# One order of matmuls for every unit of weights in a two-block transformer kernel

## The reference, cut to what matters

```
first_block:  h += hybrid_mixer(rmsnorm(h))          # h @ w_in, SSD, convolutions, @ w_out
              h += memory_cross_attention(rmsnorm(h)) # w_q, w_k, w_v, w_o
              h += (silu(n @ w_gate) * (n @ w_up)) @ w_down        # n = rmsnorm(h), D_FF = 5632
second_block: x += concat(pool, hyena, gmlp)(n @ w_in_2) @ w_out_2
              up = dwconv3(n @ ffn_w_up_2);  gate, val = split(up)
              x += (silu(gate) * val) @ ffn_w_down_2
return rmsnorm(x)
```

## Time and profile before

| | us |
|---|---|
| median of three executions | 2719.59 (2719.28 to 2724.88) |
| profiled execution, its own time | 2724.14 |
| span in the profile, first to last instruction | 2722.4 |
| TensorE busy with matmuls | 2656.2, 14978 of them |
| VectorE busy | 1924.6 |
| ScalarE busy | 1495.8 |

### The profile page before, as it was taken

How to read it: one execution, slowest core, us unless ns; L and a number is a source line. 1 busy time by engine, 2 the same in 40 slices (tenths; PEclk the granted TensorE clock), 3 DMA queues, 4 the chain that set the end, 5 groups by cost and what they waited for, 6 DMA issues and landing times.

```text
span 2722.4 us, 38546 instructions
## 1 busy us (share of the span) xinstructions
PE 2656.2 (98%) x14978; PEld 2286.7 (84%) x14978; DVE 1924.6 (71%) x2916; ACT 1495.8 (55%) x2307; POOL 388.7 (14%) x391
## 2 busy tenths in 40 slices
PE   7999999999998999999999999999999999999997
PEld 7888888888887888888888878888888888888886
DVE  8776777777787665656565679687876767676775
ACT  6555566768555444444444456545555555555554
POOL 3011100403411000010101033011101010101012
PEclk9999999999998999999999999999999999999998
DMA  6555566656554555666666656536566666666663
GB/s 247 173 180 182 184 191 193 186 182 183 174 175 134 168 162 171 186 187 188 189 186 187 190 161 209 162 124 185 178 193 188 187 189 189 186 187 187 190 178 118
DMA packets 135838, 490.76 MB, mean 180 GB/s; under 512 B 15207, under 2 KB 15528, under 8 KB 135656
## 3 DMA queue, kind: packets, MB, share of 16 engines
q1 hardware_dynamic: 135656, 488.31, 59.2%
HBM read 486.12 MB, written 2.13 MB: 179 GB/s over the span
## 4 chain that ended last, share of the span: by engine, by line
PE 87%; DVE 8%; ACT 2%; issue 2%; DMA 0%; DVEq 0%; ACTq 0%; SPq 0%
PE ps L715 32%; PE ps L733 24%; PE ps L716 16%; PE ps L730 12%; DVE wl L1218 3%; ACT wh L936 1%; DVE hT L1218 1%; DVE X L1224 1%; PE ps L872 0%; PE ps L905 0%; DVE A L1224 0%; DVE T L1224 0%; DVE R L1218 0%; DVE Gf L1218 0%; DVE T L1218 0%
## 5 line engine op out<-in xcount | busy, mean ns | idle before, releaser
L1218 DVE TENSOR_TENSOR wl<-raw,wh 128x1024 fp32r<-128x1024 f32 x902 | 1139.7, 1268 | 723.9 <-ACT wh L936 722.6
L936 ACT ACTIVATE wh<-raw 128x1024 fp32r<-128x1024 f32 x902 | 952.4, 1059 | 967.2 <-PE ps L716 536.2
L733 PE MATMUL ps<-X,wh 128*128 128x512 f32 x2816 | 860.1, 396 | 2.8 <-DVE hT L1218 2.8
L715 PE MATMUL ps<-XG,wh 128*128 128x512 f32 x2304 | 827.3, 403 | 29.7 <-DVE hT L1218 16.4
L715 PE MATMUL ps<-X,wh 128*128 128x512 f32 x2032 | 725.2, 401 | 2.0 <-DVE wl L1218 1.3
L716 PE MATMUL ps<-XG,wl 128*128 128x256 f32 x2304 | 650.4, 282 | 0.0
L716 PE MATMUL ps<-X,wl 128*128 128x256 f32 x2032 | 568.7, 280 | 0.0
L730 PE MATMUL ps<-X,wl 128*128 128x256 f32 x2816 | 564.6, 281 | 0.0
L715 PEld LDWEIGHTS ps<-XG,wh 128*128 128x128 f32 x2304 | 436.8, 190 | 142.9 <-DVE hT L1218 21.8
L733 PEld LDWEIGHTS ps<-X,wh 128*128 128x128 f32 x2816 | 481.5, 189 | 71.9 <-issue 4.7
L730 PEld LDWEIGHTS ps<-X,wl 128*128 128x128 f32 x2816 | 484.6, 189 | 61.5
(11 more groups left out here) (172 smaller groups left out, 1313.6 us busy)
## 6 DMA issues: line engine op xcount, KB each, us to landing
raw<-in_w_gate SPq DMA_DIRECT2D x176, 512.0 KB, 3.7
raw<-in_w_down SPq DMA_DIRECT2D x176, 512.0 KB, 3.7
raw<-in_w_sc SPq DMA_DIRECT2D x96, 512.0 KB, 4.2
raw<-in_w_up SPq DMA_DIRECT2D x88, 512.0 KB, 3.7
raw<-in_w_val SPq DMA_DIRECT2D x88, 512.0 KB, 3.7
raw<-in_w_zx SPq DMA_DIRECT2D x80, 512.0 KB, 3.8
raw<-in_w_in SPq DMA_DIRECT2D x68, 512.0 KB, 3.8
raw<-in_w_osc SPq DMA_DIRECT2D x32, 512.0 KB, 3.7
```

The source lines that it names most:

```text
L715: e.matmul(bank(c, i)[:, :], W1, x, start=st and kk == 0, stop=False)
L733: t = e.matmul(bank(c, i)[:, :], wh[:, b0:b0 + 128], X[:, kx * 512:kx * 512 + 512], start=st and kk == 0, stop=sp and n == ends[i])
L936: return e.activation(out, in_, ACT.Copy, scale=scale)
L1218: return e.tensor_tensor(out, a, b, op)
```

## The change

In every unit, per tile of K: the 512-column matmuls of its banks, and then the 256-column ones (order 1 above). `ORDERS` and `ORDER_OF` are gone, and gate and up columns wait tile by tile like the others. The `v` columns, with three 256-column matmuls, keep their order; `dt` has one bank, so its order is the same.

```diff
             for kk in range(c.kn):
                 X, kx, s, n = xtile(c, g * c.kn + kk)
-                if kk == 0 or c.kind not in ("gate", "up"):
-                    w.wait_ge(s, xtile(c, g * c.kn + c.kn - 1)[3] if c.kind in ("gate", "up") else n)
+                w.wait_ge(s, n)
                 x = X[:, kx * 512:(kx + 1) * 512]
-                if c.kind in ("gate", "up"):
-                    continue
-                for i in range(nb):
-                    b0 = (u % NW) * UN + kk * c.w
-                    if c.kind != "v":
-                        W1, W2 = wh[:, b0 + 128 * i:b0 + 128 * i + 128], wl[:, b0 + 128 * i:b0 + 128 * i + 128]
-                        e.matmul(bank(c, i)[:, :], W1, x, start=st and kk == 0, stop=False)
-                        t = e.matmul(bank(c, i)[:, 0:256], W2, x[:, 0:256], start=False, stop=sp and kk == c.kn - 1)
...
-            if c.kind in ("gate", "up"):
-                order = ORDERS[ORDER_OF[c.i]]
-                ends = {i: n for n, (kk, i, low) in enumerate(order)}
-                for n, (kk, i, low) in enumerate(order):
...
+                else:
+                    for i in range(nb):
+                        e.matmul(bank(c, i)[:, :], wh[:, b0 + 128 * i:b0 + 128 * i + 128], x, start=st and kk == 0, stop=False)
+                    for i in range(nb):
+                        t = e.matmul(bank(c, i)[:, 0:256], wl[:, b0 + 128 * i:b0 + 128 * i + 128], x[:, 0:256], start=False,
+                                     stop=sp and kk == c.kn - 1)
             t.then_inc(mm, 1)
```

More of the change, by code:

```diff
@@ L383, in schedule @@
     return at
[L387 to L394, removed]
 PLAN = schedule()
@@ L705, in unit @@
                 X, kx, s, n = xtile(c, g * c.kn + kk)
-                if kk == 0 or c.kind not in ("gate", "up"):
-                    w.wait_ge(s, xtile(c, g * c.kn + c.kn - 1)[3] if c.kind in ("gate", "up") else n)
+                w.wait_ge(s, n)
                 x = X[:, kx * 512:(kx + 1) * 512]
-                if c.kind in ("gate", "up"):
-                    continue
-                for i in range(nb):
-                    b0 = (u % NW) * UN + kk * c.w
-                    if c.kind != "v":
-                        W1, W2 = wh[:, b0 + 128 * i:b0 + 128 * i + 128], wl[:, b0 + 128 * i:b0 + 128 * i + 128]
-                        e.matmul(bank(c, i)[:, :], W1, x, start=st and kk == 0, stop=False)
-                        t = e.matmul(bank(c, i)[:, 0:256], W2, x[:, 0:256], start=False, stop=sp and kk == c.kn - 1)
-                    else:
-                        W1, W2 = wh[:, b0:b0 + 256], wl[:, b0:b0 + 256]
+                b0 = (u % NW) * UN + kk * c.w
+                if c.kind == "v":
+                    W1, W2 = wh[:, b0:b0 + 256], wl[:, b0:b0 + 256]
+                    for i in range(2):
                         xh, xl = x[:, i * 128:i * 128 + 128], x[:, 256 + i * 128:384 + i * 128]
```

## The result

The changed kernel took 2710.5 us (median of five, 2707.5 to 2710.9) against 2719.3 for the kernel before (five, 2717.6 to 2724.9): a ratio of 0.9962, with a 95% interval of 0.995 to 0.9975. Run again twice, it took 2707.2 and 2708.9 beside 2720.6 and 2718.8 (ratios 0.996, [0.9948, 0.9973], and 0.9957, [0.9945, 0.997]). All together, 16 executions have a median of 2708.5 and 56 of before one of 2719.5: 11 us, 0.4%. The forecast of 2704 lay 6.5 us too low, inside the range of 2696 to 2713 but just outside the likeliest case's own range of 2698 to 2710. Its profiled execution took 2710.54 us (span 2708.7), 13.6 less than that of before, where 16.0 was forecast.

The account below looks back on a forecast made before the run. TensorE's matmul spacing was taken as the bound. Gains of 11.2 us outside gate/up and 4.8 in gate/up sum to 16.0, turning the profiled 2724.1 into 2708.1; 4.5 less for unprofiled executions gives 2704, with an 8-in-10 range of 2696 to 2713.

Parts of the forecast that it names:

- the likeliest case: Whole kernel: the forecast of 2704 us itself, chance 0.80, with its own range of 2698 to 2710 for level mix and clock.
- What bounds the kernel: Whole kernel: TensorE is busy 98% of the span, so time is the sum of start-to-start spacings of matmuls.
- Order 1's pace: Four-unit gate/up columns of the kernel before: 2.787 us a unit, one level, taken to hold in all changed units.
- the 4.8: Gate/up units: sum of the gains from giving all of them the new order, 4.8 us.
- the other 494 gain 0.023 each: 11.2 us: Units outside gate/up where TensorE is the bound: from a mean of 2.810 to 2.787 us, 11.2 us in all.
- 4.5 less, so 2703.6: Whole kernel: unprofiled median lies 4.5 us below the profiled execution, so the profiled forecast of 2708.1 becomes 2703.6.
- two more or fewer: Idle places: two more or fewer half-clock stretches, 1.6 us each, move the time by 3 us.
- Only gate/up gains: Rival: down, out and mixer columns gain nothing, leaving 4.8 us; time 2714.8, chance 0.08.
- order doesn't matter: Rival: the levels belong to the stretch, not the order of matmuls; time stays at 2719.6, chance 0.04.
- slower by a high level: Rival: the new order also has a high level, 2.840 us a unit; time 2734 at the old share, chance 0.04.
- The bigger gain: Rival: the new order throughout finds 2.773 us a unit; some 850 units save 0.013 more, 11 us; 2693, chance 0.04.
- Order 0's mix: Undisturbed units outside gate/up, 512 and 256 columns alternating: 249 high at 2.827 us, 119 low at 2.7735, mean 2.810.

Follow-up runs that it names:

- the parts done alone: Two kernels against the one before: new order only outside gate/up, 2711.4 us (ratio 0.9968); new order and tile-wise waits only in gate/up, 2712.0 us (0.9974).
- order 0 alone: Against the changed kernel: every unit alternates 512- and 256-column matmuls, one bank after the other; median of 12 executions 2716.7 us, profiles 2730.8 and 2714.3.

## Why the prediction came out as it did

**What bounds the kernel** was right: the two long stretches stayed full and gave 8.2 of the 13.6 us; the rest came from undisturbed units elsewhere.

**Order 1's pace carried over** to other columns, operands and neighbours, as forecast: 2.787 everywhere, one level, also in the parts done alone. Taken unit by unit between the two first profiles, the 365 undisturbed units outside gate/up saved 8.5 us, 0.023 each as forecast, and the 323 in gate/up 4.7 us of the 4.8.

**The mis-sized term** is "the other 494 gain 0.023 each: 11.2 us". Nearly all of them did. Beside the undisturbed ones, some 110 run a foreign matmul, or the unit ahead of them does, without a wait and at full clock, and they saved 2.5 us, 0.023 each. What was left out are some 15 units with a wait or a half-clock stretch in one of the two profiles: together they lost 3.6 us, where 0.3 of gain was counted. Some 1.7 of that are longer waits, 0.57 of it in one unit near 721 us, for the residual add: TensorE gets there earlier and the add comes no sooner. The rest is the clock: a unit near 94 us met a half-clock stretch that before had not (1.57 us), and near 1810 us a stretch moved and a wait grew (0.35). The other way, a unit near 711 us, priced at nothing, was spared one that before had (1.55). So 16.0 became 13.6 between profiles.

**The other step that was off** is "4.5 less, so 2703.6": it carried the distance between before's profiled execution and its median over to the changed kernel. That distance was before's clock, 0.992 in the profiled execution and 0.994 in its middle ones. The changed kernel has 0.992 in its middle ones too, so its first profile lay on its median. At 0.992 the forecast for the profiled execution, 2708.1, meets a mean of 2709.4. The two errors, 2.4 and 4.5 us, together stayed inside the range, but the range's own term for the clock was too small: "two more or fewer" allowed 3 us, and executions of one kernel differ by six such stretches, 10 us.

**The rivals.** Only gate/up gains, order doesn't matter, and slower by a high level fell, by the down windows at 2.787. The bigger gain fell too: no stretch of order 1 went to 2.773. The waits per tile were worth nothing. Order 0's mix, which the first term took from one profile, came out nearly the same in before (119 and 113 low), partly by luck, as stretches changed both ways. It did not in order 0 alone (99 and 325 of some 690).

What stays open: why order 0 has two levels, and what decides after a disturbance which one a stretch takes; and why the changed kernel's executions had the lower clock. Order 1 outside gate/up alone had a mean of 0.9939 in eleven executions, and order 1 in gate/up alone 0.9936 in seven, so neither part brings it by itself; 16 executions don't exclude chance.

## What to carry to other kernels

Where matmuls of two sizes alternate, read the pace from start to start in windows of whole columns, for each order: equal work took 2.773, 2.787, 2.793 or 2.827 us a unit. Pairs of equal size gave one level in every profile, though not the shortest. A single profiled execution can lie 10 us from another of the same kernel by the clock alone, so compare the granted clock at the idle places before taking a difference of profiles or carrying one to a median, and compare executions of two kernels at the same mean clock. A gain per unit held for units beside a foreign matmul as well; where TensorE waits, it was eaten by a longer wait.

## What the hardware showed that was not expected

The pace of a stream 512, 256, 512, 256 columns has two levels, 0.3467 and 0.3533 us a pair, that hold for tens or hundreds of units (237 in one stretch), and that a single unit of another order can exchange. A stream 512, 512, 256, 256 has one, 0.3484, in every profile. The Trainium skill's page "TensorE: Matmul & The Clock Gate", section "Back-to-back issue gap", gives the warm gap of an isolated matmul by its columns alone, and by it all orders would be alike; for a stream with a weight load per matmul it has no rule on the order of sizes either. The runs disagree with the first: 2.773 to 2.827 us for the same columns.

The half-clock stretches at idle places come and go between executions of the same program. In the third profile of the changed kernel there is none from 836 to 876 us; in the first, the clock averages 0.87 there. The same page, in "What's actually happening", says that the monitor does not start with the kernel, so that an execution may meet it in another phase; these two profiles agree with that.
